# Value products and router of an encoder kernel, issued as two halves of 64 weight columns

## The reference, cut to what matters

```python
# one group of layer 0 (4 heads of 64), window blocks of queries against keys
s = einsum('nbqhd,nbkhd->nbhqk', qb, kw) * dh ** -0.5
p = exp(where(mask, s, NEG_INF) - logsumexp)
o = einsum('nbhqk,nbkhd->nbqhd', p, vw)            # group value products
# memory attention, both layers
p = softmax(einsum('bshd,bmhd->bhsm', q, k) * HEAD_DIM ** -0.5)
mo = einsum('bhsm,bmhd->bshd', p, v)               # memory value products
# router, both layers
grp_logits = xt @ w_grp + b_grp                    # 4 columns
exp_logits = xt @ w_exp_router + b_exp             # 32 columns
```

## Time and profile before

| | before |
|---|---|
| median of three runs | 2389.68 us (2384.38 to 2389.80) |
| the profiled execution | 2381.76 us |
| its span | 2379.9 us |
| its mean granted TensorE clock | 0.955 |
| TensorE products busy | 2194.7 us, 92% of the span |
| VectorE, ScalarE, GpSimd busy | 33%, 19%, 14% |

### The profile page before, as it was taken

One profiled execution on the slowest core, in us unless ns is written; L12 is line 12 of the kernel. 1 busy time (PEld: TensorE's weight loads), 2 busy tenths in 40 slices (PEclk: granted clock), 3 DMA queues, 4 the chain that ended last, 5 costly groups with the idle time before them and its releaser, 6 DMA issues. The chain is left out here.

```text
span 2379.9 us, 38275 instructions
## 1 busy us (share of the span) xinstructions
PE 2194.7 (92%) x15591; PEld 1169.8 (49%) x15591; DVE 777.5 (33%) x1715; ACT 457.1 (19%) x930; POOL 338.6 (14%) x398
## 2 busy tenths in 40 slices
PE   8999998886999999999698999899599999999975
PEld 5665757554444444444454666665444444444422
DVE  2133333634121212112724656542431212112215
ACT  0030304321010101001224444431200101011011
POOL 0000000151111111113510000004211111111304
PEclk9999997996999999999799999999699999999997
DMA  9023102434999999997600000021479999999945
GB/s 354 6 70 109 41 1 103 177 125 171 384 399 385 394 388 390 395 380 304 240 21 18 1 1 1 29 96 44 201 276 386 396 391 392 385 379 393 385 174 212
DMA packets 97128, 535.54 MB, mean 225 GB/s; under 512 B 20848, under 2 KB 44688, under 8 KB 72080
## 3 DMA queue, kind: packets, MB, share of 16 engines
q1 hardware_dynamic: 78928, 492.32, 52.9%
q0 software_dynamic: 18112, 41.99, 4.9%
HBM read 511.21 MB, written 41.45 MB: 232 GB/s over the span
## 5 line engine op out<-in xcount | busy, mean ns | idle before, releaser
L839 PE MATMUL banks<-ring,arena 128*32 128x256 f32 (+3 forms) x10464 | 1334.1, 452 | 37.0 <-DMA ring<-in_exp_w_gu 13.6
L839 PEld LDWEIGHTS banks<-ring,arena 128*32 128x32 f32 (+2 forms) x10464 | 564.4, 124 | 751.2 <-issue 611.1
L839 PE MATMUL banks<-ring 128*128 128x512 f32 (+3 forms) x1232 | 342.4, 554 | 4.4 <-issue 3.0
L839 PEld LDWEIGHTS banks<-ring 128*128 128x128 f32 (+2 forms) x1232 | 169.8, 190 | 149.4 <-issue 138.7
L1859 DVE TENSOR_TENSOR arena<-arena,banks 128x384 f32<-128x384 f32 x65 | 36.0, 554 | 609.3 <-ACT arena L1417 599.6
L774 POOL DMA_INDIRECT expert_out<-arena,scatter_idx x64 | 61.3, 959 | 824.1 <-DVE arena L1868 803.9
L1417 ACT ACTIVATE arena<-banks 128x384 f32<-128x384 f32 x65 | 31.9, 491 | 735.1 <-PE banks L839 735.1
L730 POOL TENSOR_TENSOR arena<-arena,ln_gb 128x1024 f32<-128x1024 f32 x28 | 69.4, 2484 | 580.0 <-ACT arena L1382 580.0
L1865 DVE COPY arena<-banks 32x256 f32<-32x256 f32 x130 | 55.3, 426 | 280.0 <-PE banks L839 279.2
L839 PE MATMUL banks<-arena 128*64 128x128 f32 (+5 forms) x1152 | 124.1, 310 | 12.5 <-DMA arena<-in_mem_w_kv 6.4
L839 PEld LDWEIGHTS banks<-arena 128*64 128x64 f32 (+3 forms) x1152 | 109.1, 179 | 28.2 <-issue 14.7
(11 more groups left out here) (183 smaller groups left out, 1508.2 us busy)
## 6 DMA issues: line engine op xcount, KB each, us to landing
ring<-in_exp_w_gu SPq DMA_DIRECT2D x130, 2048.0 KB, 17.2
ring<-in_exp_w_down SPq DMA_DIRECT2D x65, 2048.0 KB, 22.3
ring<-in_x_t SPq DMA_DIRECT2D x6, 2304.0 KB, 16.5
moe_in<-arena POOLq DMA_DIRECT2D x16, 512.0 KB, 3.0
arena<-expert_out SPq DMA_DIRECT2D x16, 512.0 KB, 4.3
ring<-expert_out SPq DMA_DIRECT2D x16, 512.0 KB, 4.3
ring<-in_a_w_in SPq DMA_DIRECT2D x6, 1024.0 KB, 17.9
arena<-in_a_w_in SPq DMA_DIRECT2D x4, 1024.0 KB, 15.8
```

What stands on the lines that cost most here:

```text
L839: return nc.tensor.matmul(out, lhsT, rhs, start=start, stop=stop)
```

## The change

In the value products of the groups and of the memory attention, and in the router, each product of 128 weight columns becomes two of 64. The first writes partitions 0 to 63 of the result (the first 64 queries or tokens), the second partitions 64 to 127. The moving operand is the same for both. Nothing else is changed: the waits, the other engines' work, and the buffers stay.

```diff
@@ attention_step, value products of unit u-1 @@
                         for h in range(GH):
                             for c in range(nch):
-                                last = mm(ps[:, 6 + b, h * DV:(h + 1) * DV], prob_t[:, b, h * 256 + c * P:h * 256 + (c + 1) * P],
-                                          vals[:, vt + c, h * DV:(h + 1) * DV], c == 0, c == nch - 1)
+                                for q in range(0, P, 64):
+                                    last = mm(ps[q:q + 64, 6 + b, h * DV:(h + 1) * DV],
+                                              prob_t[:, b, h * 256 + c * P + q:h * 256 + c * P + q + 64],
+                                              vals[:, vt + c, h * DV:(h + 1) * DV], c == 0, c == nch - 1)
                         last.then_inc(pv, 1)
@@ router @@
                 for k in range(KT):
-                    last = mm(ps[:, 5, 256:256 + NR], XT[:, k, t * P:(t + 1) * P], w_router[:, k], k == 0, k == KT - 1)
+                    for q in range(0, P, 64):
+                        last = mm(ps[q:q + 64, 5, 256:256 + NR], XT[:, k, t * P + q:t * P + q + 64], w_router[:, k], k == 0, k == KT - 1)
                 last.then_inc(r_ps, 1)
```

## The result

| | before | after |
|---|---|---|
| median of the runs | 2388.45 us (2384.38 to 2389.80, 4 runs) | 2359.19 us (2356.31 to 2362.72, 4 runs) |
| ratio, 95% interval | | 0.988 (0.9863 to 0.9897) |
| the profiled execution | 2381.76 us | 2357.78 us |
| its span | 2379.9 us | 2355.9 us |
| mean granted clock | 0.955 | 0.961 |

The changed kernel is faster by 29.3 us by the medians and by 24.0 us by the two profiled executions. The forecast of 2360 us lies 0.8 us from the median.

What follows compares the result with a forecast made beforehand. TensorE's products, busy 92% of the span, were taken to bound the kernel, with the softmax loop close. Terms 10.8 + 2.5 + 0 + 15.9 = 29.2 us saved gave 2360 us against the median, range 2350 to 2368, chance 0.61.

Steps and rivals of the forecast that it cites:

- The pair: Value products and router: two half products of 64 weight columns load at once and cost 0.059 us together, against 0.112.
- the turns: Rival: the two halves' weight loads take turns, a pair costs 0.115 us, time 2400 us; chance 0.08.
- the feeding floor: Rival: TensorE can't be fed faster than a record each 0.056 us; time 2384 us; chance 0.14.
- the first rival: The rival of halves' loads in turns: a pair at 0.115 us, time 2400 us; chance 0.08.
- The period in groups 0 and 1: Memory attention of layer 1: unit period falls from 3.82 to 3.5 us, saving 2.1 us over group 0's six intervals.
- rival of a loop that stays at 3.8: Softmax loop doesn't tighten, only a stage's last two units gain: 23 us saved, time 2367 us; chance 0.10.
- a clock that falls inside these groups: Rival: more idle time drops TensorE to 1.2 GHz in groups 0 and 1, time 2381 us; chance 0.07.
- The tail of groups 0 and 1: Behind the last transposes, two units of value products stand alone and shrink from 3.68 us, saving 1.5 us.
- Group 2: Waits for stores and exponentials, then TensorE binds at 1.2 GHz: 2.5 us saved, bounds 0 and 4.
- Memory attention of layer 0: Nothing counted, because the merge's load lands only at 437.1 us; bounds 0 and 1.5 us.
- Output projections: Shorter routers in both layers: 2.65 early, 0.45 at router 4, 4.85 at routers 5 to 7; 7.95 us each.
- The experts and the sum: Experts unchanged, shifting earlier as a whole with their weight requests; all terms together save 29.2 us.

Runs made afterwards that it cites:

- The control: The kernel before the change, with only SyncE's loads of the stored groups issued ahead of the gain, shift and router weight loads: 2387.70 us, ratio 0.9992.
- the quarters: Four products of 32 weight columns in place of the changed kernel's two of 64, in value products and router: 2354.47 us, ratio 0.9854 against the kernel before.

## Why the prediction was right

**The pair.** Forecast 0.059 us for two halves; measured 0.058 to 0.059 (from one unit alone to two together 32 records more cover 0.94 us, 2.09 less 1.15). The borders came out too: 1.08 us from the value products to the scores, and 0.09 more from the transposes' start to the value products (1.02, where it was 0.93), make 1.17 against the 1.19 of the forecast. The order of the halves is what makes it (1.90 us a unit apart, 1.15 together). The two rivals that denied it are refuted: the turns by that run, the feeding floor by one record in 0.012 us.

The Trainium skill, "TensorE: Matmul & The Clock Gate", The mechanism, lets a load overlap running products only in another row group. The halves share all rows, and the time would have been that of the first rival by it; the runs speak against it, with 1.15 us for what takes 1.90 in turns.

**The period in groups 0 and 1.** Forecast 3.5 from the softmax loop; six intervals cover 21.10 us (163.76 less 142.66), 3.52 each, from 3.36 to 3.79. The transposes wait for the exponentials now, as the argument of two periods in 6.95 us said. The rival of a loop that stays at 3.8 is refuted, and so is that of a clock that falls inside these groups (transposes of eight still cover 1.09).

**The tail of groups 0 and 1.** This step was mis-sized. The value products behind the last transposes did shrink by 1.59 (3.68 to 2.09), but from the last transposes to the projection it is 4.57 us after 5.27, a gain of 0.70 and not 1.5. I had said that the projection waits for that end; it waits for ScalarE's copy, and the copy for a store. The idle time before the projection went from 0.66 to 1.46 us. The term took no account of that wait, though it stood there before the change. In the run without it the projection follows the value products at once. In the memory attention of layer 1, where no such wait stands, the forecast of 3.6 was met (3.58).

**Group 2.** Forecast 2.5, with a bound of 4; 3.49 measured. Here I had luck with the clock, as TensorE's timeline after shows:

```profile
387.00 0.69 PE L839 MATMUL banks<-arena 128*64 128x65 f32 x16
388.80 0.97 PE L935 MATMUL banks<-ident,arena 128*128 128x128 f32 x4 [1.12 <-ACT arena L1365]
389.70 2.00 PE L839 MATMUL banks<-arena 128*64 128x65 f32 x32
```

Sixteen records at 387.00 still cover 0.69, as at 2.4 GHz. The four transposes behind them begin to stretch (0.97), and the last 32 records run at 1.2 GHz; in the earlier trace rows the transposes were at that level from 385.85 on.

**Memory attention of layer 0.** Forecast nothing; the merge's shift is even 0.85 less than that of the stage's start, and the load is what it waits for. The two runs with the load ahead confirm that it was the load.

**Output projections.** Forecast 7.95 each; 9.25 and 8.18. Of the 9.25, 3.90 lie before router 4's sum (forecast 3.1: the sum stood at 522.26 and stands at 510.22, a shift of 12.04) and 5.35 behind it (forecast 4.85). The 5.35 are not made as I had them. I had all three late routers at 1.2 GHz, each on the path with 1.6 to 1.7. Router 5 came to run at 2.4 and ends 2.47 us earlier (its sum at 529.63 and 515.12 is a shift of 14.51 after 12.04), but 1.11 of that went in VectorE's longer step, so router 6 starts only 1.36 earlier by it (534.71 and 521.31, a shift of 13.40). Router 6 saves 1.67 at the lower clock, as forecast, and the transposes behind it give back some 0.15. Router 7 saves 2.47, 0.8 of it because it ran at the upper clock. So the sum of this term is near by luck in part: a clock that was too good and a step on VectorE that was not foreseen. In layer 1 it is again 5.35 behind router 4's sum (1677.58 and 1657.33), with routers 5 and 7 at the upper clock as in layer 0.

**The experts and the sum.** 29.15 from the stages against the forecast 29.2: the errors of the terms cancel (groups 0 and 1 -1.7, group 2 +1.0, memory 0 -0.85, output projections +1.5), and that it is met to 0.05 is luck. I had carried the whole sum through the experts. Between the two profiled executions 5.15 are given back, 1.65 and 1.6 of it in the experts and 1.77 ahead of the latent attention. There, behind transposes that partly run at the lower clock in after, sixteen records of a projection cover 9.38 us (from 1244.94) where they cover 7.39 before (from 1260.90). But the profiled execution of before is 6.7 us below its median and that of after 1.4 below its own; that difference of 5.3 is the difference of 29.3 and 24.0. The control differs from before by 3.5 us in experts that its edit does not touch. That the 5.15 are such scatter fits this, and is not shown, for I have one trace of each kernel.

## What to carry to other kernels

Where an fp32 matmul's moving operand is shorter than its weights are wide (here 65 and 36 columns against 128), the weight load was the cost, and splitting the weight columns into two pieces that stand next to each other nearly halved it (0.112 to 0.058 us); all first pieces before all second ones gave about a quarter of the kernel's gain (7.6 us of 29.3 by the medians). By the quarters, split until the load of a piece is no longer than the stream of the moving operand (64 columns for 65 moving, 32 for 36). Then look at what the freed engine runs into: here the softmax loop, the store of a stage buffer and a load that had been just in time, of which the last two could be moved away for another 5.8 us by the medians.

## What was not expected

- Records can follow each other every 0.012 us (64 router records of 32 columns in 0.77 us); the densest ones of before were 0.056 apart.
- A half alone costs 0.058 us, as much as a pair side by side. All first halves before all second halves still cost no more than whole products (64 records in 3.41 us, before 32 in 3.68), since at each border the records of both halves run together.
- The length of the work on TensorE moves where the clock changes: router 7 ran at the lower clock before and with the router only, and at the upper one in the full change, with the same idle time of 0.83 us before it in all three.
- A router that ends 2.47 us earlier brought the next one forward by 1.36 only, since VectorE's step between them took 2.34 us for 1.23.
